# mLSTM gate rows spread by one-pass matmuls from split operands, and attention sums in alternating PSUM banks

## The reference, cut to what matters

```
li = gate_chunks(i_pre)                      # (4 heads, 8 chunks of 64)
lf = log_sigmoid(gate_chunks(f_pre))
b  = cumsum(lf)
m_t = maximum(max(log_d), b + m_in)          # stabiliser
scores = einsum(qc, kc) * exp(log_d - m_t)   # needs b - m_t along the row axis
inter  = exp(b + m_in - m_t)                 # scales the queries
h = num / maximum(abs(den), exp(-m_t))
...
p = softmax(q @ k.T / 16)                    # 4 heads, 512 x 256
o = p @ v                                    # 256 channels a head
x = x + o @ w_o
```

## Time and profile before

| what | value |
|---|---|
| time, median of 3 runs | 2040.15 us (2038.14, 2040.15, 2040.28) |
| time of the profiled execution | 2040.14 us |
| its span, first to last instruction | 2038.3 us |
| PE busy | 2013.6 us (99%) |
| DVE, ACT, POOL busy | 45%, 45%, 52% |
| share of PE in the chain that ended last | 90% |
| mean granted TensorE clock | 0.996 |

### The profile page before, as it was taken

The page is one execution under the profiler, slowest core; times in us unless marked ns, Lnnn a source line. Parts: engine busy times, 40 slices in busy tenths (PEclk is TensorE's granted clock), DMA queues, the critical chain, the costliest instruction groups (busy, mean ns, idle before and its releaser), DMA issues.

```text
span 2038.3 us, 32893 instructions
## 1 busy us (share of the span) xinstructions
PE 2013.6 (99%) x12983; PEld 1667.1 (82%) x12983; DVE 924.5 (45%) x1400; ACT 908.0 (45%) x1551; POOL 1060.5 (52%) x1364
## 2 busy tenths in 40 slices
PE   8999999999999999999999999999999999999998
PEld 7788878878996888888897887888788788888887
DVE  6665788845223321212257577887540432211112
ACT  6744544335445442423356536243454544433323
POOL 4564443746752455545466436357377345546451
PEclk9999999999999999999999999999999999999999
DMA  5422223323431333233333232223333223333332
GB/s 172 115 75 73 79 77 82 92 88 95 144 114 53 93 99 98 95 98 98 96 86 91 70 83 79 79 74 98 99 123 126 68 88 93 99 98 94 98 99 72
DMA packets 202677, 191.11 MB, mean 94 GB/s; under 512 B 25658, under 2 KB 200220, under 8 KB 202140
## 3 DMA queue, kind: packets, MB, share of 16 engines
q1 hardware_dynamic: 202524, 189.02, 31.5%
HBM read 184.77 MB, written 3.15 MB: 92 GB/s over the span
## 4 chain that ended last, share of the span: by engine, by line
PE 90%; DVE 5%; ACT 3%; DMA 1%; issue 1%; POOL 0%; SPq 0%; DVEq 0%; ACTq 0%
PE gemm L596 82%; PE mix L596 7%; DVE work L1633 2%; DMA w_raw<-in_w_in_dram 1%; DVE work L1637 1%; DVE work L1642 1%; DVE work_split L1642 0%; ACT work L1557 0%; ACT w_hi L1173 0%; DVE work L2071 0%; DVE s_phases L1633 0%; DVE merged L1633 0%; DVE s_small L2201 0%; DVE gate_t L1642 0%; ACT work_split L1312 0%
## 5 line engine op out<-in xcount | busy, mean ns | idle before, releaser
L589 POOL TENSOR_TENSOR w_lo<-w_raw,w_hi 128x256 fp32r<-128x256 f32 (+1 forms) x680 | 551.8, 812 | 950.4 <-ACT w_hi L1173 950.0
L596 PE MATMUL gemm<-work_split,w_hi 128*128 128x512 f32 (+1 forms) x2048 | 602.4, 378 | 1.7 <-POOL w_lo L590 1.7
L596 PE MATMUL gemm<-h_hi,w_hi 128*128 128x512 f32 (+1 forms) x1456 | 576.6, 396 | 0.3 <-POOL w_lo L590 0.3
L596 PE MATMUL gemm<-h_lo,w_hi 128*128 128x512 f32 (+1 forms) x1456 | 567.2, 390 | 0.0
L596 PE MATMUL gemm<-h_hi,w_lo 128*128 128x512 f32 (+1 forms) x1456 | 567.0, 389 | 0.0
L590 POOL TENSOR_TENSOR w_lo<-w_raw,w_hi 128x256 fp32r<-128x256 f32 (+1 forms) x680 | 556.1, 818 | 0.0
L1173 ACT ACTIVATE w_hi<-w_raw 128x512 fp32r<-128x512 f32 (+1 forms) x680 | 384.3, 619 | 248.1 <-DMA w_raw<-in_mlp_w_dram 185.9
L596 PEld LDWEIGHTS gemm<-work_split,w_hi 128*128 128x128 f32 x2048 | 376.5, 189 | 75.0 <-issue 5.0
L596 PE MATMUL gemm<-work_split,w_lo 128*128 128x512 f32 (+1 forms) x1024 | 385.7, 377 | 0.0
L596 PEld LDWEIGHTS gemm<-h_hi,w_hi 128*128 128x128 f32 (+1 forms) x1456 | 272.8, 187 | 63.1 <-issue 4.6
L596 PEld LDWEIGHTS gemm<-h_hi,w_lo 128*128 128x128 f32 (+1 forms) x1456 | 272.7, 187 | 58.4
(11 more groups left out here) (289 smaller groups left out, 1696.4 us busy)
## 6 DMA issues: line engine op xcount, KB each, us to landing
w_raw<-in_mlp_w_dram SPq DMA_DIRECT2D x256, 256.0 KB, 2.7
w_raw<-in_w_in_dram SPq DMA_DIRECT2D x224, 256.0 KB, 2.7
w_raw<-in_xattn_w_kv_dram SPq DMA_DIRECT2D x64, 256.0 KB, 2.8
w_raw<-in_w_branch_dram SPq DMA_DIRECT2D x32, 256.0 KB, 2.7
w_raw<-in_w_out_dram SPq DMA_DIRECT2D x32, 256.0 KB, 2.7
w_raw<-in_xattn_w_q_dram SPq DMA_DIRECT2D x32, 256.0 KB, 2.8
w_raw<-in_xattn_w_o_dram SPq DMA_DIRECT2D x32, 256.0 KB, 2.7
work<-in_x_dram SPq DMA_DIRECT2D x4, 512.0 KB, 6.2
```

The lines of the kernel that those rows point to most:

```text
L589: pool.tensor_tensor(lo[:, 0:half], raw[:, 0:half], hi[:, 0:half].bitcast(F32), ALU.subtract)
L596: return pe.matmul(o, w, a, start=start, stop=stop, skip_group_check=True)
```

## The change

The three gate quantities are split like the weights: ACT copies the rounded rows into a new fp32r operand `GROWS` on 128 partitions, DVE puts the remainders 32 partitions further down. `AROWS` (512 columns) holds rounded R(24) in partitions 0 to 3, its remainder in 32 to 35, rounded R(28) in 64 to 67, its remainder in 96 to 99; `BROWS` (256 columns) holds b - m_t by chunk parity in the same way. All other rows are zero. `head_sel` and `pair_sel` repeat the 0/1 rows at those partitions, so that one matmul over all 128 partitions adds rounded part and remainder. The selection matrices are copied from the constants into `GROWS` in every layer, since this memory is that of the S5 phases. The constants grow by 256 columns. In the attention `out_pair` is M[0:2] for heads 1 and 3, a gemm set for heads 0 and 2; the waits follow.

```
+        GROWS = nc.alloc_sbuf_tensor_at("gate_rows", [P, 2048], F32R, offset=phases_at)
+        AROWS, BROWS = GROWS[:, 0:512], GROWS[:, 512:768]
+        head_sel = GROWS[:, 768:1280].rearrange("p (h a m) -> p h a m", h=4, a=2)
+        pair_sel = GROWS[:, 1280:1792].rearrange("p (n j m) -> p n j m", n=2, j=2)
...
         def out_pair(h):
-            return M[0:2] if h == 2 else G[psum_set("o1")[0]]
+            return M[0:2] if h % 2 else G[psum_set("o1")[0]]
...
# PE
                 pe.wait_ge(*of_layer(head_rs, 8))
+                pe.wait_ge(*of_layer(ms["rows_split"], 2))
                 for j in range(2):
-                    mm(M[1 + j][:, :], pair_sel[0:4, j, :], R(24)[0:4, 0, :]).then_inc(ms["ib_done"], 1)
+                    mm(M[1 + j][:, :], pair_sel[:, 0, j, :], AROWS).then_inc(ms["ib_done"], 1)
                     if j:
                         pe.wait_ge(*of_layer(ms["rows_out"], 1))
-                    mm(M[3 if j == 0 else 0][:, :], pair_sel[32:36, j, :], R(28)[32:36, 0, :]).then_inc(ms["aw_done"], 1)
+                    mm(M[3 if j == 0 else 0][:, :], pair_sel[:, 1, j, :], AROWS).then_inc(ms["aw_done"], 1)
...
+                pe.wait_ge(*of_layer(ms["rows_split"], 4))
                 for hp in range(2):
                     for j in range(2):
-                        for a in range(2):
-                            i = mm(M[hp][64 * a:64 * a + 64, j * 256:j * 256 + 256], head_sel[0:4, 2 * j + hp, :], bm[:, :, a, :])
+                        i = mm(M[hp][:, j * 256:j * 256 + 256], head_sel[:, 2 * j + hp, :, :], BROWS)
...
                     if k == 0:
                         pe.wait_ge(*of_layer(at["pt_ready"], 2 * h + 2))
-                        if h in (1, 3):
-                            pe.wait_ge(*of_layer(at["osplit_ready"], h + 1))
+                        if h == 1:
+                            pe.wait_ge(*of_layer(at["p_exp"], 12))
+                        if h >= 2:
+                            pe.wait_ge(*of_layer(at["osplit_ready"], 2 * h - 2))
...
# ACT
-                do(act.activation(R(28)[32:36, 0, :], R(21)[0:4, 0, :], ACT.Exp, scale=-1.0), ms["stack_ready"])
+                do(act.activation(R(28)[64:68, 0, :], R(21)[0:4, 0, :], ACT.Exp, scale=-1.0), ms["stack_ready"])
                 y_split(1)
+                do(act.activation(AROWS[0:4, :], R(24)[0:4, 0, :], ACT.Copy), ms["stack_ready"])
+                do(act.activation(AROWS[64:68, :], R(28)[64:68, 0, :], ACT.Copy), ms["stack_ready"])
+                do(act.activation(R(22)[64:68, 0, :], R(22)[0:4, 0, :], ACT.Copy))
+                for a in range(2):
+                    rows = slice(64 * a, 64 * a + 4)
+                    bm = R(22)[rows, 0, :].rearrange("p (t a c) -> p t a c", a=2, c=CH)[:, :, a, :]
+                    do(act.activation(BROWS[rows, :].rearrange("p (t c) -> p t c", c=CH), bm, ACT.Copy), ms["stack_ready"])
                 act.preload_act_table_set(EXP_SET)
...
# DVE
                 states(gl)
+                do(dve.memset(GROWS[:, 0:1280].bitcast(F32), 0.0))
+                for a in range(2):
+                    rows = slice(64 * a, 64 * a + 64)
+                    do(dve.tensor_copy(head_sel[rows, :, a, :], const("head_sel")[rows].rearrange("p (h m) -> p h m", h=4)))
+                do(dve.tensor_copy(GROWS[:, 1280:1792], const("pair_sel")))
                 silu_of(2)
...
                 branch_out(1, gl.O, gl.SQ, 1, "gla_norm", silu_gate(gl))
+                for n, (r, a) in enumerate(((24, 0), (28, 64))):
+                    dve.wait_ge(*of_layer(ms["stack_ready"], 2 + n))
+                    stt(AROWS[a + 32:a + 36, :], R(r)[a:a + 4, 0, :], 1.0, AROWS[a:a + 4, :].bitcast(F32), ALU.mult, ALU.subtract,
+                        ms["rows_split"])
+                for a in range(2):
+                    dve.wait_ge(*of_layer(ms["stack_ready"], 4 + a))
...
+                    stt(halves(BROWS[low, :]), R(22)[rows, 0, :].rearrange("p (t a c) -> p t a c", a=2, c=CH)[:, :, a, :], 1.0,
+                        halves(BROWS[rows, :]).bitcast(F32), ALU.mult, ALU.subtract, ms["rows_split"])
```

More of the change, by code:

```diff
@@ L61 @@
 for _name, _n in (("ident", 128), ("head_mean", 128), ("mean", 128), ("ones", 64), ("neg", 64), ("reset", 512),
-                  ("pair_sel", 256), ("head_sel", 256), ("parity", 2)):
+                  ("pair_sel", 512), ("head_sel", 256), ("parity", 2)):
     CCOL[_name] = (_at, _n)
@@ L88, in shape_constants @@
         head[h, h, :] = 1.0
-    put("pair_sel", np.concatenate([pair.reshape(4, 256), np.zeros((28, 256)), pair.reshape(4, 256)]))
-    put("head_sel", head.reshape(4, 256))
+    both = np.zeros((P, 2, 256), np.float32)
+    for n in range(2):
+        for at in (64 * n, 64 * n + 32):
+            both[at:at + 4, n] = pair.reshape(4, 256)
+    put("pair_sel", both.reshape(P, 512))
+    four = np.zeros((4, 32, 256), np.float32)
+    four[:, 0:4] = head.reshape(4, 256)
+    put("head_sel", four.reshape(P, 256))
     put("parity", np.stack([(r // 16) % 2 == 0, (r // 16) % 2 == 1], 1).astype(np.float32))
@@ L167 @@
     hg_exp=8, hg_kt_ready=2, mlstm_cin_ready=4, s5_sin_ready=1, head_squares=6, head_factors=12, y_hi=8, gl_exp=8,
-    mlstm_mth_ready=4, mlstm_a1=2, gl_kt_ready=1, s5_u_ready=2, mlstm_stack_ready=1, mlstm_rows_out=5,
+    mlstm_mth_ready=4, mlstm_a1=2, gl_kt_ready=1, s5_u_ready=2, mlstm_stack_ready=5, mlstm_rows_split=4, mlstm_rows_out=5,
     mlstm_mex_ready=1, mlstm_mbd_ready=1, s5_xp_zero=2, s5_ct_ready=2, s5_bt_ready=4, s5_sq=2, s5_tanh=2,
@@ L231, in build @@
         ones64, neg_mask, reset = const("ones"), const("neg"), const("reset")
-        pair_sel = const("pair_sel").rearrange("p (j m) -> p j m", j=2)
-        head_sel = const("head_sel").rearrange("p (h m) -> p h m", h=4)
         parity = const("parity")
@@ L347, in build @@
                    "ib_done", "ib_ready", "mex_done", "mex_v", "mex_ready", "mqk_done", "matt_ready", "mbd_ready",
-                   "mkt_done", "mkt_ready", "mkv_done", "ms_ready", "mo_done", "mh_ready", "stack_ready")
+                   "mkt_done", "mkt_ready", "mkv_done", "ms_ready", "mo_done", "mh_ready", "stack_ready", "rows_split")
         ms = {n: sem("mlstm_" + n) for n in m_names}
@@ L914, in _ @@
                 pe.wait_ge(*of_layer(ms["rows_out"], 3))
-                bm = R(22)[0:4, 0, :].rearrange("p (t a c) -> p t a c", a=2, c=CH)
+                pe.wait_ge(*of_layer(ms["rows_split"], 4))
                 for hp in range(2):
                     for j in range(2):
-                        for a in range(2):
-                            i = mm(M[hp][64 * a:64 * a + 64, j * 256:j * 256 + 256], head_sel[0:4, 2 * j + hp, :], bm[:, :, a, :])
+                        i = mm(M[hp][:, j * 256:j * 256 + 256], head_sel[:, 2 * j + hp, :, :], BROWS)
                     i.then_inc(ms["mex_done"], 1)
@@ L1984, in _ @@
                 branch_out(1, gl.O, gl.SQ, 1, "gla_norm", silu_gate(gl))
+                for n, (r, a) in enumerate(((24, 0), (28, 64))):
[4 more added lines that the diff above has]
+                    dve.wait_ge(*of_layer(ms["stack_ready"], 4 + a))
+                    rows, low = slice(64 * a, 64 * a + 4), slice(64 * a + 32, 64 * a + 36)
+                    halves = lambda ap: ap.rearrange("p (t c) -> p t c", c=CH)
+                    stt(halves(BROWS[low, :]), R(22)[rows, 0, :].rearrange("p (t a c) -> p t a c", a=2, c=CH)[:, :, a, :], 1.0,
+                        halves(BROWS[rows, :]).bitcast(F32), ALU.mult, ALU.subtract, ms["rows_split"])
                 do(dve.tensor_copy(pr(17), Ur[:, S5_T, :]))
```

## The result

The changed kernel takes 2046.54 us (median of 7 runs, 2043.76 to 2047.99), the kernel before 2039.91 us on the same chip (7 runs, 2036.47 to 2040.28): a ratio of 1.0033, 95% interval 1.0023 to 1.0042. It is slower by a third of a per cent. The forecast was 2041.1 with a range up to 2043.0, so it was wrong: 5.4 us too low in the median, 4.15 us in the profiled execution (2045.25 us, span 2043.5).

A forecast was written before the change was run, and what follows sets the result against it. PE, busy 2013.6 of 2038.3 us, was taken as the bound. Matmuls and ACT's wait +0.86, attention 0, old clock falls -3.10, new falls +3.20: +0.96 on 2040.14 gives 2041.1 us, range 2037.5 to 2043.0.

The forecast's parts named there:

- Spreading matmuls and ACT: mLSTM branch: matmuls save 1.23 us, but ACT's later `MAW` copy makes PE wait 3.0; `branch1_0` starts 1.82 later per layer.
- head_sel: Eight small matmuls become four of 256 columns, 1.87 us to 0.48, saving 1.39 us in each layer.
- The clock: Two profiled falls in layer 0 go (-3.10 us); the spreading wait brings one per layer, 1.60 each (+3.20).
- The fall at the small products: Layer 0 behind `head_sel`: the profiled clock fall, 1.50 us, was expected not to come again.
- DVE pays nothing on the path: Ahead of `mex_done`: DVE's added instructions fit its idle stretches of 8.51 and 4.70 us, costing nothing.
- Attention: The 0.75 us wait before out(1) goes, but out(2) waits for ACT: worth nothing, bounds 0 and -0.75 a layer.
- The rivals: Fewer falls (one 0.25, none 0.09); ACT not delaying `MAW` (0.10); attention keeping 0.75 us a layer (0.05); longer falls (0.06).
- Rival 4: At the spreading wait each clock fall lasts twice as long, 3.20 us each, giving 2044.3 us; chance 0.06.

The follow-up runs named there:

- act_only: Kernel before plus ACT's five added copies alone, results unused, at the same place; 2051.59 us, ratio 1.0062 to before.
- after_xp: Kernel after with the first half of DVE's `XP` work moved in front of `branch_out(0)`; 2042.84 us, ratio 1.0016 to before.
- dve_2us_behind_mex: Kernel before plus three unused DVE instructions a layer (2.15 us) in front of `phases(16)`, behind `mex_done`; 2045.10 us, ratio 1.0032 to before.
- fourth_late: Kernel after, attention as before, with the fourth spreading matmul moved behind `branch1_0`; 2041.46 us, ratio 1.0012 to before.
- dve_rem_only: Kernel before plus DVE's four remainders (and a memset of their operands), unused, where the change has them; 2044.90 us, ratio 1.0027 to before.
- dve_rem_late: Kernel before plus the same four unused DVE remainders as dve_rem_only, but behind `merge(1, 0)`; 2039.91 us, ratio 1.0004 to before.
- fourth_and_b_late: fourth_late with ACT's three b - m copies moved behind the `MAW` copy and their remainders behind `merge(1, 0)`; 2042.14 us, ratio 1.0013 to before.
- fourth_b_xp: The same kernel as fourth_and_b_late, profiled once more, with no change to `XP`; 2044.01 us, one run.

## Why the prediction was wrong, point by point

**Spreading matmuls and ACT.** Right in mechanism, place and size: wait 3.01 us forecast as 3.0, the `MAW` copy at 270.30 instead of 270.12, `branch1_0` 4.31 us behind the first spreading matmul instead of 4.0. The account has +2.17 and +2.20 for +1.82, because the fourth matmul took 0.33 us instead of 0.23 (the granted clock was still 1.00 there) and ACT was 0.18 later than summed. `act_only` shows that these five copies are the cause.

**`head_sel`.** -1.40 for -1.39, in each layer. But the prediction counted it as time of the kernel. Half of it, 0.70 us, brings the mask additions forward; the other half lies beside DVE's chain and came back as a wait.

**The clock.** In both layers it fell at the wait for `MAW`, as forecast, at +1.44 for +1.60 in layer 1. It fell just behind the wait, though: over 267.4 to 270.4 us, in the wait, it is 1.00, and over 270.8 to 274.3 it is 0.51. The three kernels with the 3 us wait fell there in both layers, the five with the fourth matmul late in neither. The view by stretches gives its length, the busy times of PE, PEld, DVE, ACT and POOL, the granted clock, and the DMA's share and GB/s. Over 268 to 276 us the clock is 0.79, so part of it was spent at 1.2 GHz:

```profile
268.00:276.00 8.00, 5.64 (x18) 4.50 (x19) 7.61 (x12) 5.39 (x11) 8.00 (x12) 0.79 0.04 13
286.00:292.00 6.00, 6.00 (x91) 5.21 (x90) 4.89 (x7) 1.91 (x3) 0.00 (x0) 1.00 0.19 48
```

The fall at the small products is gone, also as forecast (second row), and none of the eight kernels with the new `head_sel` has it in either layer. But the forecast took 1.50 us for it from one execution. Of the nine experiments that left `head_sel` alone, two had it in layer 0 and three in layer 1; with the kernel before that is 6 of 20 places, so on average it is worth about 0.9 us for both layers (an estimate: 6 x 1.5 / 10). And where DVE is the later engine, PE's time saved here is waited for again.

**DVE pays nothing on the path: the step that failed.** The two rows of the transposes of `XP` are 1.98 + 1.83 = 3.81 us of the 4.2 by which the account misses the forecast, and 0.35 of them is the wait at 478 us named below. The prediction looked at the idle marks in front of `mex_done` (8.51 and 4.70 us), found DVE's additions smaller, took DVE off the path, and so counted all that PE saves from there on, 1.39 us a layer at `head_sel` and 1.50 for the fall, as time of the kernel. For the additions themselves the reading even held: 3.73 and 3.71 us of idle time are left in front of the mask additions. Two things were missing.

First, it never asked what DVE does behind `mex_done`: a chain of 73 us whose end PE already waited 0.74 us for in layer 1. PE waits there for the difference of two delays, its own and the chain's. In layer 0 the mask additions come 1.20 us later than before and DVE ends `XP` 1.28 later, while PE would be there 0.94 earlier (the sum of its rows in the account, down to the fall); DVE was done 0.78 us ahead of PE there before, and is 1.9 behind it after. In layer 1 it is 3.90 and 4.82 against 3.28, of which 1.04 is brought in from layer 0. So the wait for ACT delays both alike, and what PE saves beside the chain, half of `head_sel` and in layer 0 the fall, it waits at the end; in layer 1 the 0.92 that the chain grew comes on top. `after_xp` shows it by taking the wait away, `dve_2us_behind_mex` by making it longer.

The chain of layer 0 had idle time, 5.25 us in front of `branch_out(0)`, of which 0.84 gave way, before and then after:

```profile
345.75 0.75 DVE L1642 SCALAR_TENSOR_TENSOR work<-work,params_all 128x512 f32<-128x512 f32 x1 [5.25 <-ACT work L1291]
```

```profile
346.51 0.90 DVE L1660 SCALAR_TENSOR_TENSOR work<-work,params_all 128x512 f32<-128x512 f32 x1 [4.41 <-ACT work L1302]
```

It also had 2.43 us at the copies for `mkv_done`. They are gone, because DVE's short S5 phase products came 1.06 us later and GpSimd's splits, first at 304.22 instead of 305.16, 0.94 earlier, so that the two now meet. A 64-column product takes 0.66 us instead of 0.23. In layer 1 some of these products met the splits already before, and now all do, which is most of the 0.92. A product of layer 0 after, and the same one before:

```profile
308.53 0.66 DVE L1651 TENSOR_TENSOR s_phases<-work 128x64 f32<-128x64 f32 x1
```

```profile
304.71 0.23 DVE L1633 TENSOR_TENSOR s_phases<-work 128x64 f32<-128x64 f32 x1
```

Second, an instruction was priced by its own length and not by what it pushes aside. In the kernel after this stayed hidden behind the larger wait, and it came out as soon as that wait was taken away (`fourth_late`).

**Attention.** Worth nothing, as forecast, by the wait that was named.

**The rivals.** None named a chain of DVE. Rival 4 came nearest in time (2044.3) for a wrong reason: in the kernel after the falls did not last twice as long, at 0.79 over eight us in each layer. Falls of about that length do occur, in both layers of `act_only` and in layer 1 of `after_xp`.

What stays open: at 478 us PE loses 0.35 us in all eight kernels with the new rows and in `dve_rem_only` and `dve_rem_late`, and nothing in the other seven. It waits 1.2 us for a weight from GpSimd there instead of 0.9; why that one comes later is not known. Nor was `head_sel` changed alone, so its 1.4 us are known from the account only.

## What to carry to other kernels

An idle mark ahead of a hand-over says nothing about slack behind it: follow each engine that receives the hand-over to the next place where somebody waits for it, and count a saving only up to the point where another engine becomes the later one. When two delays run side by side, the larger one hides the smaller, so removing one alone gives little; test each by itself, as extra work in the old kernel. Short DVE instructions with two SBUF inputs belong where GpSimd is idle.

## What the runs showed of the hardware that was not expected

- A DVE sum of 128x8 took 0.17 us alone and 0.65 while GpSimd ran weight splits of 0.74 us; a product of 128x64 took 0.23 and 0.66. GpSimd's own instructions stayed at 0.70 us apart. So most of a chain of short instructions ran at a quarter to a third of its speed.
- A plain fp32 matmul on four rows by 512 columns cost 2.00 us alone behind a wait in which the clock fell, 1.39 where it fell 0.7 us behind the wait, and 0.54 in the packed sequence before.
- The first 90 us of 17 nearly equal programs differ by up to 2.8 us between executions, those of one and the same program by 2.2 (`fourth_and_b_late` and `fourth_b_xp`), and a fall of the clock at a given place comes in some executions and not in others (1.5 us each). Behind such a place all differences stay constant to a few hundredths, so single stretches can be compared far more sharply than whole times.
